# A decoder's last stage: plain fp32 token gather, eighteen weight slots, and a new order at the gate

## The reference

```python
x = x + hier_moe(rmsnorm(x, norm_ffn_g), routers, w_gate_e, w_up_e, w_down_e)
hp = rmsnorm(x, norm_ple_g)
x = x + (p @ w_ple) * sigmoid(hp @ w_ple_gate)
return rmsnorm(x, final_norm_g)
```

## Time and profile before

| | |
|---|---|
| median of 3 runs | 1020.57 us |
| profiled execution, its own time | 1019.16 us |
| its span, first to last instruction | 1017.6 us |
| mean granted clock of TensorE | 0.990 |
| TensorE busy with matmuls | 955.7 us (94%) |
| VectorE, ScalarE, GpSimd busy | 636.0, 536.8, 84.2 us |
| transfers | 224.58 MB, mean 221 GB/s |

### The profile page before, as it was taken

The page is one execution under the profiler, slowest core; times in us unless marked ns, Lnnn a source line. Parts: engine busy times, 40 slices in busy tenths (PEclk is TensorE's granted clock), DMA queues, the critical chain, the costliest instruction groups (busy, mean ns, idle before and its releaser), DMA issues.

```text
span 1017.6 us, 14997 instructions
## 1 busy us (share of the span) xinstructions
PE 955.7 (94%) x5635; PEld 733.5 (72%) x5635; DVE 636.0 (63%) x1392; ACT 536.8 (53%) x976; POOL 84.2 (8%) x97
## 2 busy tenths in 40 slices
PE   6999899999999999999999999989899999887776
PEld 5777588888888877688888888768676655443345
DVE  3779768999846576769999846666785212110056
ACT  5757667666635565667666636765642111110055
POOL 0100001121100311001211101100000000000000
PEclk9999999999999999999999999999999999999979
DMA  8934346655565544356565563404759999999951
GB/s 270 383 128 125 103 126 197 196 168 204 204 190 186 181 151 125 93 165 199 167 199 201 178 193 124 151 21 167 278 219 370 403 418 419 421 422 421 421 201 42
DMA packets 99359, 224.58 MB, mean 221 GB/s; under 512 B 9535, under 2 KB 64210, under 8 KB 86994
## 3 DMA queue, kind: packets, MB, share of 16 engines
q1 hardware_dynamic: 99122, 223.04, 61.3%
q10 hardware_dynamic: 160, 0.53, 0.1%
HBM read 222.50 MB, written 1.05 MB: 220 GB/s over the span
## 4 chain that ended last, share of the span: by engine, by line
PE 76%; SPq 7%; DVE 6%; DMA 6%; ACT 3%; issue 2%; DVEq 0%; ACTq 0%
PE ps L560 72%; SPq L2971 6%; PE ps L564 3%; DMA ring<-in_w_ple_gate_dram 3%; DMA ringx<-in_w_up_e_dram 2%; DVE wl L1972 1%; DVE smb L1986 1%; DMA ring<-in_w_in_even_dram 1%; SPq L2974 1%; ACT wh L1428 0%; ACT hh L1425 0%; DVE pb L1977 0%; SPq L2956 0%; DVE hl L1982 0%; ACT pb L1425 0%
## 5 line engine op out<-in xcount | busy, mean ns | idle before, releaser
L1972 DVE TENSOR_TENSOR wl<-ring,wh 128x1024 fp32r<-128x1024 f32 (+3 forms) x212 | 269.0, 1270 | 107.1 <-ACT wh L1428 105.8
L1428 ACT ACTIVATE wh<-ring 128x1024 fp32r<-128x1024 f32 (+3 forms) x212 | 222.1, 1051 | 106.3 <-PE ps L560 101.2
L560 PE MATMUL ps<-hx,wh 128*128 128x512 f32 (+1 forms) x720 | 245.0, 389 | 0.1
L560 PE MATMUL ps<-hx,wl 128*128 128x256 f32 x704 | 194.6, 277 | 0.0
L560 PEld LDWEIGHTS ps<-hx,wh 128*128 128x128 f32 x720 | 134.0, 188 | 30.5 <-issue 0.6
L560 PEld LDWEIGHTS ps<-hx,wl 128*128 128x128 f32 x704 | 132.2, 188 | 0.0
L560 PE MATMUL ps<-wh,hh 128*128 128x512 f32 (+3 forms) x192 | 79.7, 415 | 3.2 <-DVE wl L1972 3.1
L2916 POOL TENSOR_TENSOR fs<-fs,rt 128x256 f32<-128x256 f32 x44 | 52.5, 1214 | 356.0 <-ACT fs L1425 356.0
L560 PE MATMUL ps<-ring,xg 128*32 128x256 f32 (+1 forms) x576 | 73.3, 381 | 7.8 <-DMA ring<-in_w_up_e_dram 5.7
L560 PE MATMUL ps<-wl,hh 128*128 128x512 f32 (+3 forms) x192 | 74.9, 390 | 0.0
L560 PE MATMUL ps<-wh,hl 128*128 128x512 f32 (+3 forms) x192 | 72.9, 387 | 0.0
(11 more groups left out here) (318 smaller groups left out, 1692.6 us busy)
## 6 DMA issues: line engine op xcount, KB each, us to landing
ring<-in_w_up_dram SPq DMA_DIRECT2D x88, 512.0 KB, 4.8
ring<-in_w_down_dram SPq DMA_DIRECT2D x22, 1024.0 KB, 5.1
ring<-in_w_up_e_dram SPq DMA_DIRECT2D x20, 1024.0 KB, 13.2
ring<-in_w_down_e_dram SPq DMA_DIRECT2D x18, 1024.0 KB, 20.9
ring<-in_w_gate_e_dram SPq DMA_DIRECT2D x16, 1024.0 KB, 13.4
ringx<-in_w_gate_e_dram SPq DMA_DIRECT2D x14, 1024.0 KB, 12.4
ring<-in_w_in_odd_dram SPq DMA_DIRECT2D x12, 1024.0 KB, 5.1
ringx<-in_w_down_e_dram SPq DMA_DIRECT2D x12, 1024.0 KB, 20.7
```

Source lines behind the costliest of these rows:

```text
L560: return e.matmul(o, l, r, start=start, stop=stop)
L1428: return e.activation(o, i, ACT.Copy)
L1972: return e.tensor_tensor(o, a, b, op)
```

## The change

Three things, in the stages of the experts and of the gate:

1. The tokens are gathered from x itself: `xk[:, t, :, k]`, every eighth fp32 value of a token's row, is the stationary operand, `S_` becomes plain fp32, and each slice takes 2 plain fp32 matmuls. `xh`, `xl`, `x_lo`, `w10`, `wt10` and `two_parts` are gone; `slot_rows` multiplies by `w3` in plain fp32 (5 columns), and VectorE reads its bank out straight into `wsl` and `rsl`.
2. NX goes from 6 to 8: eighteen slots.
3. At the end, `ysh` and `ysl` of group 9 come first; ScalarE does `gate_hi(0)` and `(1)` behind them and the other six behind `hh`, VectorE all eight `gate_lo` behind `hl`. The two outputs of n = 0 are computed together, part by part (all `hh*wh`, then `hl*wh`, then `hh*wl`), each part with its own waits; then (1 after 0) the two of n = 1. The outputs are read out as (0,0), (1,0), (0,1), (1,1), and ScalarE's square of x's tile 0 waits for the third of them.

```diff
@@ -27,7 +27,7 @@
 NU = 9
-NX = 6
+NX = 8
@@ -190,17 +190,16 @@
         wroom.close()
-        r1, S_, ScT, xg, ringx, ysh, ysl, xh, xl, smr, wsl, rsl, w10, wt10 = opened(
-            ("S_", [P, 2, 2, S], F32R), ("ScT", [P, 4, S], F32R), ("xg", [P, 2, 8, S], F32), ("ringx", [P, NX, UW], F32),
-            ("ysh", [P, DM], F32R), ("ysl", [P, DM], F32R), ("xh", [P, 2, DM], F32R), ("xl", [P, 2, DM], F32R),
-            ("smb", [P, 3, 384], F32), ("wsl", [P, 16], F32), ("rsl", [P, 16], F32),
-            ("w10", [P, 2, 10, 10], F32R), ("wt10", [P, 2, 2, 10], F32))
+        r1, S_, ScT, xg, ringx, ysh, ysl, smr, wsl, rsl = opened(
+            ("S_", [P, 2, 2, S], F32), ("ScT", [P, 4, S], F32R), ("xg", [P, 2, 8, S], F32), ("ringx", [P, NX, UW], F32),
+            ("ysh", [P, DM], F32R), ("ysl", [P, DM], F32R),
+            ("smb", [P, 3, 384], F32), ("wsl", [P, 16], F32), ("rsl", [P, 16], F32))
         hT = xg[:, 1, :, :]
         r1.close()
 
-        r1, gfl, _, gw2, gw3, hhp, hlp, sg, gw0 = opened(
+        r1, gfl, _, gw2, gw3, hhp, hlp, gw0, sg = opened(
             ("gfl", [P, DM], F32), ("gap0", [P, DM], F32), ("gw2", [P, 2, 1024], F32R), ("gw3", [P, 10, 1024], F32R), *HH,
-            ("sg", [P, 2, 1024], F32), ("gw0", [P, 4, 1024], F32R))
+            ("gw0", [P, 4, 1024], F32R), ("sg", [P, 2, 1024], F32))
...
@@ -1283,16 +1281,15 @@
                     for k in (2 * m, 2 * m + 1):
-                        for n_, (v, t) in enumerate(((xh, 0), (xh, 1), (xl, 0), (xl, 1))):
-                            w = mm(b[:, (k % 2) * S:(k % 2 + 1) * S], v[:, t, k * P:(k + 1) * P], S_[:, g % 2, t, :],
-                                   n_ == 0, n_ == 3)
+                        for t in range(2):
+                            w = mm(b[:, (k % 2) * S:(k % 2 + 1) * S], xk[:, t, :, k], S_[:, g % 2, t, :], t == 0, t == 1)
                     w.then_inc(of(full, "xg", g, m), 1)
 
             def slot_rows(g):
                 b, b2 = take("ScT", g), take("wsl", g)
                 for j in range(4):
                     i, t = 2 * g + j // 2, j % 2
-                    w = tr(b[:, j * P:(j + 1) * P], slots_of(i, t).bitcast(F32))
+                    w = tr(b[:, j * P:(j + 1) * P], slots_of(i, t))
@@ -1301,7 +1298,7 @@
                     for t in range(2):
-                        w = mm(b2[:, 10 * j:10 * j + 10], slots_of(i, t), w10[:, t, i, :], t == 0, t == 1)
+                        w = mm(b2[:, 5 * j:5 * j + 5], slots_of(i, t), w3[:, t, i, :], t == 0, t == 1)
@@ -1382,7 +1379,6 @@
             for part in range(2):
-                q.wait_ge(s_xlo, 3 + part)
                 gather(0, part)
@@ -1402,20 +1398,31 @@
             norm_T("np2", added("moe"))
+            def gate_step(n, t, k, part):
+
+                c = 4 * n + k // 2
+                h, l = (v[:, k % 2 * 512:(k % 2 + 1) * 512] for v in gate_w[c])
+                if part == 2:
+                    q.wait_ge(w_split, c_gate[0] + c + 1)
+                elif part == 1:
+                    emptied(q, "np2", k // 2)
+                else:
+                    q.wait_ge(w_hi, c_gate[0] + c + 1)
+                    q.wait_ge(s_hh, hsplit["np2"] + k + 1)
+                v = (hhp, hlp, hhp)[part]
+                w = mm(bank[use[("gate", n), t][0]][:, :], v[:, k, t * P:(t + 1) * P], (h, h, l)[part],
+                       k + part == 0, k == 7 and part == 2)
+                if k == 7 and part == 2:
+                    w.then_inc(of(full, ("gate", n), t), 1)
+
             for t in range(2):
-                tk = slice(t * P, (t + 1) * P)
-                for n in range(2):
-                    b = claim(2 * t + n, ("gate", n), t)
-                    for k in range(8):
-                        c = 4 * n + k // 2
-                        q.wait_ge(w_split, c_gate[0] + c + 1)
-                        if t == 0 and n == 0:
-                            emptied(q, "np2", k // 2)
-                        wh_, wl_ = (v[:, k % 2 * 512:(k % 2 + 1) * 512] for v in gate_w[c])
-                        mm(b[:, :], hhp[:, k, tk], wh_, k == 0, False)
-                        mm(b[:, :], hhp[:, k, tk], wl_, False, False)
-                        w = mm(b[:, :], hlp[:, k, tk], wh_, False, k == 7)
-                    w.then_inc(of(full, ("gate", n), t), 1)
+                claim(2 * t, ("gate", 0), t)
+            for part, t, k in product(range(3), range(2), range(8)):
+                gate_step(0, t, k, part)
+            for t in range(2):
+                claim(2 * t + 1, ("gate", 1), t)
+                for part, k in product(range(3), range(8)):
+                    gate_step(1, t, k, part)
@@ -1861,15 +1868,11 @@
 
-            for n in range(2):
-                emptied(q, (2, "out"), 0, n)
-                copy(xhk[:, 0, 64 * n:64 * n + 64], xk[:, 0, 64 * n:64 * n + 64]).then_inc(s_xhi, 1)
             q.wait_ge(s_cl, CLATE)
             norm_T("nf2", hT)
             act(xg[:, 0, 0:4, :].rearrange("p k s -> p (k s)"), x[:, 0, :], ACT.Square, accum_out=st[:, 0:1]).then_inc(s_sq, 1)
             q.wait_ge(s_var, RV["nf2"])
             act(st[:, 16:18], st[:, 8:10], ACT.Sqrt).then_inc(s_std, 1)
-            copy(xhk[:, 1], xk[:, 1]).then_inc(s_xhi, 1)
@@ -1886,10 +1889,6 @@
                     evac(ScT[:, 2 * (g % 2):2 * (g % 2) + 2, :].rearrange("p a s -> p (a s)"), "ScT", g)
-                b = filled(q, "wsl", g)
-                if g >= 2:
-                    q.wait_ge(s_wsl, g - 1)
-                copy(wt10[:, g % 2, :, :].rearrange("p j c -> p (j c)"), b[:, 0:20]).then_inc(of(drained, "wsl", g), 1)
@@ -1908,7 +1907,7 @@
                     emptied(q, "gu", i - 2)
-                q.wait_ge(s_wsl, i // 2 + 1)
+                emptied(q, "wsl", i // 2)
@@ -1920,15 +1919,14 @@
                     ask(e, "ACT")
-                if i == 9:
-                    for c in range(3):
-                        gate_hi(c)
                 for n in range(2):
                     b = filled(q, "dn", i, n)
                     if i >= 1:
                         q.wait_ge(s_ys, i)
                     act(ysh[:, n * 512:(n + 1) * 512], b[:, :], ACT.Copy, scale=wsl[:, i:i + 1]).then_inc(s_yh, 1)
+            gate_hi(0)
             warm()
+            gate_hi(1)
             general(e, "ACT")
@@ -1937,7 +1935,7 @@
                     act(hhp[:, k, :], b[:, j * S:(j + 1) * S], ACT.Copy, scale=gain("np2", k)).then_inc(s_hh, 1)
-            for c in range(3, 8):
+            for c in range(2, 8):
                 gate_hi(c)
@@ -1952,9 +1950,9 @@
             q.wait_ge(s_rstd, RV["np2"])
-            for t, n in ((0, 0), (0, 1), (1, 0)):
+            for t, n in ((0, 0), (1, 0), (0, 1)):
                 sigmoid(t, n)
-            q.wait_ge(s_sgm, 2)
+            q.wait_ge(s_sgm, 3)
@@ -2641,19 +2639,10 @@
 
-            def x_lo(t, h):
-
-                q.wait_ge(s_xhi, 2 + t)
-                ks = slice(4 * h * P, 4 * (h + 1) * P)
-                tt(xl[:, t, ks].rearrange("q (k p) -> q p k", p=P), xk[:, t, :, 4 * h:4 * h + 4],
-                   xh[:, t, ks].rearrange("q (k p) -> q p k", p=P).bitcast(F32), ALU.subtract).then_inc(s_xlo, 1)
-
             q.wait_ge(s_sq, SQ["nf2"])
             ts(st[:, 8:10], st[:, 0:2], 1.0 / DM, EPS, ALU.mult, ALU.add).then_inc(s_var, 1)
-            x_lo(0, 0)
             q.wait_ge(s_std, RV["nf2"])
             rcp(rin[:, 12:14], st[:, 16:18]).then_inc(s_rstd, 1)
-            x_lo(0, 1)
...
@@ -2695,12 +2683,11 @@
                     evac(ScT[:, 0:2, :].rearrange("p a s -> p (a s)"), "ScT", g)
+                v, r = filled(q, "wsl", g)[:, 0:10].rearrange("p (j c) -> p j c", c=5), P // len(members[2 * g])
+                for h in range(len(members[2 * g])):
+                    cp(wsl[r * h:r * h + r, 2 * g:2 * g + 2], v[r * h:r * h + r, :, h])
+                cp(rsl[:, 2 * g:2 * g + 2], v[:, :, 4]).then_inc(of(drained, "wsl", g), 1)
                 emptied(q, "wsl", g)
-                v, r = wt10[:, g % 2, :, :], P // len(members[2 * g])
-                own.inc(tt(rsl[:, 2 * g:2 * g + 2], v[:, :, 4], v[:, :, 9], ALU.add))
-                for h in range(len(members[2 * g])):
-                    w = tt(wsl[r * h:r * h + r, 2 * g:2 * g + 2], v[r * h:r * h + r, :, h], v[r * h:r * h + r, :, 5 + h], ALU.add)
-                w.then_inc(s_wsl, 1)
...
@@ -2782,13 +2762,12 @@
             own.inc(cp(w3[:, :, :, 4], rin[:, 12:14].unsqueeze(2).to_broadcast([P, 2, 10])))
-            own.inc(cp(w3[:, :, 0:3, 0:2], wt[:, :, 0:6].rearrange("p t (i c) -> p t i c", c=2)))
-            two_parts(0, 3)
+            cp(w3[:, :, 0:3, 0:2], wt[:, :, 0:6].rearrange("p t (i c) -> p t i c", c=2)).then_inc(s_wt, 1)
+            q.wait_ge(s_wt, 1)
             own.inc(of_both(keyp[:, :, NS:8], 0, 2, k12))
             select(1)
             slot_rows(0)
-            own.inc(of_both(w3[:, :, 3, 0:2], 0, 2, w12))
-            two_parts(3, 4)
+            of_both(w3[:, :, 3, 0:2], 0, 2, w12).then_inc(s_wt, 1)
@@ -2798,9 +2777,6 @@
```

(19 more changed lines are left out.)

## The result

Four runs of the changed kernel have a median of 1028.55 us (1027.41 to 1029.36), four of the kernel before beside them 1019.56. The ratio is 1.0088, with a 95% interval of 1.0074 to 1.0102: the change costs about 9.0 us. The profiled execution took 1029.36 us, its span is 1027.8 us. The prediction was 1021.7 us, on the line of "no change". The time lies inside the range, at its upper end, and on the slower side, to which 0.32 was given. The likeliest case did not come.

What follows compares the result with a forecast made beforehand. TensorE was taken to bound it to 820 us, transfers from 824, then a serial tail. Stream +5.0 (TensorE +10.8, slots -5.0, some slack) and tail -3.9 gave +1.1: 1021.7 us on the medians' scale, range 1013 to 1029.

Steps and rivals of the forecast that it cites:

- The likeliest case: Whole kernel: forecast as summed, stream +3.6 to +5.8 and clock held, 1020.3 to 1022.5 us; chance 0.40.
- Slots, -5.0: Weight stream: two more units of 2.49 us load ahead in idle transfer time, moving the stream's end by -5.0 us.
- Gather, halves of 3.6 and a first pair of 7.2 us: TensorE's gather in plain fp32: a half takes 3.6 us (+1.6), the first pair 7.2 (+2.9).
- this rival (chance 0.14): Gather: strided weight loads slower by more than 1.9 set the pace; 1025.3 us at 2.2, 1035 at 3; chance 0.14.
- Copies removed: nothing back: Ahead of the gather: dropping the `xl` and `xh` copies gives nothing back on the path.
- `slot_rows` +0.5: TensorE's `slot_rows`: four fp32r matmuls become eight instructions, at most 0.12 us each, +0.5 us.
- Stream +5.0 (3.6 to 5.8): Weight stream: TensorE's 10.8 us of delay less 5.0 for slots, with some slack, shifts it by +5.0 us.
- Scatter right behind `down(9)` at the full clock: Tail: with `ysh` ahead of `gate_hi`, the scatter runs from 973.3 to about 975.8 us at the full clock.
- `hh` 6.8 us sooner: Tail, ScalarE: `hh` starts at 978.9 us against 985.73, counted in old times, a gain of 6.8 us.
- A pause of 2.5 us after four gate matmuls: Tail, TensorE: after four gate matmuls a pause of 2.5 us, as `gate_hi(2)` and `(3)` stand behind the eight `hh`.
- Clock falls in the tail (chance 0.22, +2.3): Gate products: TensorE falls to the lower clock, about 11 matmuls slow, +2.3 us, giving 1024.0; chance 0.22.
- Tail -3.9: Tail: the last sigmoid starts at 1005.9 us against 1009.78, counted in old times, a gain of 3.9 us.

Runs made afterwards that it cites:

- sixteen slots: The changed kernel with 16 weight slots in place of 18; ratio to the kernel before 1.0147.
- small gate weights: The changed kernel with only 64 of 512 columns of each gate weight block loaded; one run, 1023.74 us.
- contiguous loads: The changed kernel with the gather's weights taken as 128 neighbouring columns of x, not every eighth; ratio to the kernel before 1.0063.
- old end: The changed kernel with the gate's end in the order of before, plain fp32 gather and 18 slots kept; ratio to the kernel before 1.0071.
- short block: The changed kernel with TensorE's part of the unexecuted fallback cut from 32 experts to one; ratio to the kernel before 1.0039.
- woven end: The kernel before with the gate's new order, TensorE's jump ahead of `gate_up(9)`, and `gate_hi(1)` to `(3)` between pairs of `hh`; ratio 0.9959, 1015.34 us.
- gather alone: The kernel before with the plain fp32 gather straight from x, keeping its 16 slots and its end; ratio 1.0116.
- early jump: The kernel before with the gate's new order and TensorE's jump over the fallback moved ahead of `gate_up(9)`; ratio 0.9980.
- woven change: The changed kernel (plain fp32 gather, 18 slots) with the early jump and the woven end; ratio to the kernel before 1.0040.

## Why the prediction was right or wrong

The time lies in the range, 0.5 us from its end, but not by the forecast's reasons: the stream was off by a mis-sized term and the tail by a step that wasn't in the sum. That it fell inside is luck.

- **Slots, -5.0.** Right in mechanism. Measured 6.0 us by the ratios. In the two traces without the lower clock at 748 us (sixteen slots, and small gate weights with eighteen) the stream ends at 976.38 and 970.20, 6.2 us apart.
- **Gather, halves of 3.6 and a first pair of 7.2 us.** Too small: 4.0 and 7.7. The step that failed is the load of strided weights, taken at a factor of 1.6 from VectorE's rows (0.19 us), "no cost". A load's record includes latency: `slot_rows` puts contiguous loads of 192 ns through at one in 0.12 us (8 in 0.95). The strided ones, 335 ns long, come at one in 0.24 to 0.25, a factor of 2.0 to 2.1 in pace, just past the 1.9 from which the rival decides. So this rival (chance 0.14) came, near its milder price: 3.6 us for the factor 2.2, 2.5 measured by the ratios and 1.3 in the traces. The prediction's 0.213 us as the least for such a matmul was a little low by its own row (12 in 5.23 us are 0.436 each, half of that 0.218); contiguous loads gave 0.219. With contiguous loads the stream ends 5.6 us late in the trace (968.91 against 963.34), beside a forecast of +5.0.
- **Copies removed: nothing back.** Right. The gather still started behind TensorE's own `ppT` products.
- **`slot_rows` +0.5.** Held: 0.95 us against 0.59 of a pass with the latency, +0.4.
- **Stream +5.0 (3.6 to 5.8).** It was +7.2 by the old end's ratio, outside the forecast's bounds, and 6.9 in the traces (970.20 with small gate weights against 963.34). `gate_up(0)` at 764.6 rather than 762 is mostly the lower clock at 748 us: where that was absent, with small gate weights, it is 762.98. The starved stretch at 832 to 836 rather than near 831 is the same miss in both.
- **Scatter right behind `down(9)` at the full clock.** Right (983.07, as the last `down(9)` matmul ends).
- **`hh` 6.8 us sooner.** Wrong in the changed kernel, 2.2, because of a step that the sum didn't have: the jump over the fallback that stands between the scatter and the transposes. The short block shows 7.0 without it. Its trace was there: 0.65 us "<-issue" ahead of the transposes, an idle that I took as small and fixed. It was the visible end of a jump of 4.4 us, made while eight matmuls ran slowly. When I let them run fast and in two halves as they came, I took its cover away, moved it in among the gate weights' transfers, and costed both at nothing.
- **A pause of 2.5 us after four gate matmuls.** It came as 1.08 us here, as the four matmuls themselves ran at the lower clock (2.06 us), and as 1.91 once the jump was out of the way.
- **Clock falls in the tail (chance 0.22, +2.3).** In the change the clock fell for another reason, the idle of 5.06 us. As described, with the jump out of the way, the rival came true in both runs: 4.14 us against 2.56 for ten matmuls, 1.6 us. With the clock held by the woven end the gain was 4.2 us on the kernel before. That is near the -3.9 of the forecast, but by another order.
- **Tail -3.9.** Measured +1.7 to +3 by the ratios, +1.4 in the trace (47.8 against 46.4). This is the larger part of the error: of the 7.9 us between +1.1 and +9.0, 2.2 lie in the stream and 5.6 in the tail (1.7 + 3.9), rounding left aside. No rival named it; the time stayed within the range because that reached out for slow loads, which brought only 2.5 us of it.

What stays open: the lower clock at 748 to 751 us. It shows in the traces of the changed kernel, the gather alone, the short block, partly the old end, and the early jump (with before's gather). It doesn't show in those of the kernel before and of the other seven, four of them with the new gather (sixteen slots, contiguous, small gate weights, the woven change). So it is no property of the gather. Ahead of it TensorE runs, in all thirteen traces, 32 matmuls of 36 columns over some 3.7 us (743.58 in the changed kernel); in five of them the clock falls at their end or, with the old end, in their midst. Why in those five wasn't found, nor how much of it is in the medians. Nor is it settled what TensorE does in the 2.4 to 2.8 us between the instruction packet and its next matmul. The small gate weights were one run.

## What to carry to other kernels

A small idle "<-issue" ahead of a block that a branch skips is the end of a hidden cost, so ask how long the instructions in front of it run before making them faster or releasing them one by one; a long skipped block belongs where the engine waits for data in any case, and even there count its idle and the clock behind it (up to 1.5 us here). The profile's queues named "instruction" show when the code came. Check what a strided stationary operand does to the load from the engine's own load rows, not from another engine's, and reckon with a factor of 2 in pace. A gain that an order promises at the full clock is paid only if the pauses in it are short too: spread the producer's other work between its results.

## What the runs showed of the hardware

- TensorE's jump over the long fallback costs 5.06 to 5.18 us of idle behind the scatter while gate weights are being transferred (the changed kernel and the three others with the new end and the whole block), 2.26 us when they are an eighth of the size, and nothing over a block of one expert. Ahead of `gate_up(9)`, under full transfers, it was 2.56 to 2.86 us of idle in four traces, each followed by the lower clock (0.50 in 950 to 952 us with the early jump).
- A 16 KB packet of the queue "q8 instruction" passes 2.4 to 2.8 us before TensorE goes on behind a long jump, in twelve traces. Behind the gate weights it came 2.8 us after the last scatter matmul had started, without them 0.3 us.
- A plain fp32 weight load of 128x128 is 190 ns long from contiguous columns and 335 ns with a stride of 32 bytes, and a gather instruction of 256 columns takes 0.219 and 0.241 us in the first pair. The contiguous load is hidden, the strided one sets the pace.
- Pauses of 1.07 and 1.91 us with four matmuls between them were followed by the lower clock (0.71 in 988 to 992 us with the early jump); pauses of 0.71, 0.48 and 0.48 us were not (1.00 throughout), nor were pauses of 1.3 to 1.4 us with 32 matmuls of 256 columns between them (1.00 from 944 to 964 us in the kernel before).
